# Two-block transformer layer in split float32: interleaving the halves of the held activations, and a different column order, slot shift or weight spread in each column group of the feed-forward

## What is computed

```python
def second_block(x, mem, ...):
    h = rms_norm(x, norm_mix_g);  x = x + hybrid_mixer(h, ...)
    h = rms_norm(x, norm_x_g);    x = x + cross_attention(h, mem_n, w_xq, w_xkv, w_xo)
    h = rms_norm(x, norm_ffn_g)
    x = x + jnp.square(jax.nn.relu(h @ w_ff1)) @ w_ff2     # w_ff1 2048 x 8192, w_ff2 8192 x 2048
    return rms_norm(x, norm_final_g)
```

## Time and profile before

| | us |
|---|---|
| two timed runs | 2842.70, 2843.13 (median 2842.91) |
| the profiled execution, as timed | 2842.74 |
| its span, first to last instruction | 2841.0 |
| around the span | 1.7 |
| TensorE matmul busy | 2822.8 (99%) |
| TensorE weight load busy | 2443.4 (86%) |
| VectorE busy | 1931.6 (68%) |
| ScalarE busy | 1352.2 (48%) |

### The profile page before, as it was taken

One profiled execution on the slowest core, in us unless ns is written; L12 is line 12 of the kernel. 1 busy time (PEld: TensorE's weight loads), 2 busy tenths in 40 slices (PEclk: granted clock), 3 DMA queues, 4 the chain that ended last, 5 costly groups with the idle time before them and its releaser, 6 DMA issues.

```text
span 2841.0 us, 38749 instructions
## 1 busy us (share of the span) xinstructions
PE 2822.8 (99%) x15872; PEld 2443.4 (86%) x15872; DVE 1931.6 (68%) x2513; ACT 1352.2 (48%) x1726; POOL 59.2 (2%) x102
## 2 busy tenths in 40 slices
PE   9999999999999999999999999999999999999998
PEld 8899888888888888888888888888888888888887
DVE  7645557678766668888988875466666555656556
ACT  5433654347344436555555543444345443444434
POOL 0000210000000000000000000000000000000000
PEclk9999999999999999999999999999999999999999
DMA  7454344565555544444343445554455445554443
GB/s 279 181 191 155 142 178 178 185 241 180 196 185 200 185 167 163 148 149 143 140 149 136 159 168 204 178 193 149 148 200 191 187 179 205 190 197 181 192 190 148
DMA packets 72849, 506.66 MB, mean 178 GB/s; under 512 B 8384, under 2 KB 8512, under 8 KB 12896
## 3 DMA queue, kind: packets, MB, share of 16 engines
q1 hardware_dynamic: 71136, 497.83, 47.4%
q0 software_dynamic: 1104, 5.90, 0.6%
q10 hardware_dynamic: 432, 0.45, 0.0%
HBM read 499.95 MB, written 2.10 MB: 177 GB/s over the span
## 4 chain that ended last, share of the span: by engine, by line
PE 92%; DVE 5%; ACT 1%; issue 1%; DMA 1%; SPq 0%; POOL 0%; DVEq 0%; ACTq 0%
PE double L1376 85%; PE bank L1376 6%; DVE wlo L2076 1%; DVE cacc L2082 1%; PE bank L1379 1%; DVE cst L2099 0%; ACT whi L1734 0%; DVE AA L2082 0%; DVE cst L2076 0%; DVE cacc L2079 0%; DMA vec<-in_vec 0%; DVE Cm L2076 0%; DMA raw<-in_wall 0%; DVE Tn L2590 0%; DVE acc L2076 0%
## 5 line engine op out<-in xcount | busy, mean ns | idle before, releaser
L1376 PE MATMUL double<-AA,whi 128*128 128x512 f32 (+1 forms) x5008 | 1641.8, 380 | 3.3 <-DVE wlo L2076 3.2
L1734 ACT ACTIVATE whi<-raw 128x1024 fp32r<-128x1024 f32 x926 | 925.7, 1049 | 833.1 <-PE double L1376 794.9
L1376 PE MATMUL double<-AA,wlo 128*128 128x256 f32 (+1 forms) x4624 | 1299.1, 281 | 0.0
L2076 DVE TENSOR_TENSOR wlo<-raw,whi 128x1024 fp32r<-128x1024 f32 (+1 forms) x934 | 1101.1, 1214 | 200.6 <-ACT whi L1734 198.3
L1376 PEld LDWEIGHTS double<-AA,whi 128*128 128x128 f32 x5008 | 915.4, 188 | 180.1 <-DVE wlo L2076 5.0
L1376 PEld LDWEIGHTS double<-AA,wlo 128*128 128x128 f32 x4624 | 875.4, 189 | 1.4
L1376 PE MATMUL double<-whi,AA 128*128 128x512 f32 x1536 | 488.0, 393 | 0.5 <-DVE wlo L2076 0.5
L1376 PEld LDWEIGHTS double<-whi,AA 128*128 128x128 f32 x1536 | 288.6, 188 | 60.3 <-DVE wlo L2076 0.9
L1376 PE MATMUL double<-whi,BB 128*128 128x512 f32 x1024 | 317.0, 390 | 0.0
L1376 PE MATMUL double<-wlo,AA 128*128 128x512 f32 x768 | 299.4, 390 | 0.0
L1376 PEld LDWEIGHTS double<-whi,BB 128*128 128x128 f32 x1024 | 192.3, 188 | 40.0
(11 more groups left out here) (338 smaller groups left out, 1720.4 us busy)
## 6 DMA issues: line engine op xcount, KB each, us to landing
raw<-in_wall SPq DMA_DIRECT2D x462, 1024.0 KB, 4.8
raw<-in_wall SPq DMA_DIRECT2D x9, 256.0 KB, 6.6
X<-in_xT SPq DMA_DIRECT2D x1, 2048.0 KB, 11.3
Mm<-in_memT POOLq DMA_DIRECT2D x1, 2048.0 KB, 15.6
tmp<-rqk POOLq DMA_DIRECT2D x16, 128.0 KB, 2.2
mblk<-in_memT SPq DMA_DIRECT2D x8, 256.0 KB, 3.4
dec<-in_dec POOLq DMA_DIRECT2D x1, 1536.0 KB, 8.8
hs<-in_hsT SPq DMA_DIRECT2D x4, 272.0 KB, 5.5
```

The costliest lines, as they stand in the source:

```text
L1376: return q.matmul(out, lhsT, rhs, start=start, stop=stop, skip_group_check=True)
L1734: q.activation(hi_of(j)[:, c], raw[j % RAW][:, c], ACT.Copy).then_inc(S("w_hi"), 1)
L2076: return q.tensor_tensor(out, a, b, o)
```

## The change

Nothing is added to or taken from the list of steps. Instruction counts, shapes, waits and transfers are the same. Four things are different:

1. **Layout of the held activations.** `AA` and `BB` are of the same size, but the lo half of a k-tile now lies directly behind its hi half (1,024 bytes further, 1,088 for the 272 tokens of the first block). `AL` is the view with 272 tokens, `AT` the view with 256. The splits on ScalarE and VectorE write into these views; a copy that wrote 512 columns in one run writes two runs of 256.
2. **Slots.** A `whi` slot is 32 elements longer than a unit, a `wlo` slot 48 elements (before: 0 and 64). So the slots' starts move against each other and against `AA`.
3. **f1 groups.** `FEATURE_WAYS` gives each (b, j) but (0, 0) an order of the moving columns of the 512-column matmul, one of the 256-column matmul, a spread of the held weights (`rows`) and the two shifts of the weights in their slots. Order (s, r) walks a row of columns as `(b s r) -> s b r`: runs of r neighbouring columns, one of every s such runs in turn. Moving operand and PSUM output are walked alike, so that each sum is the same. With `rows` 2 or 8 the weights of a tile lie 2 or 8 elements apart, and the array `wall` in DRAM is laid out for that.
4. **f2 groups.** `TOKEN_WAYS` gives each (b, j) an order of the moving weight columns (all but five have one, 27 of 32) and two shifts.

```diff
+NONE = (None, (0, 0))
+PLAIN = (None, None, None, (0, 16))
+FEATURE_WAYS = {
+    (0, 1): (None, (4, 8), None, (0, 16)), (0, 2): ((4, 8), None, None, (0, 16)), (0, 3): ((4, 8), (4, 8), None, (0, 16)),
+    (1, 0): ((4, 8), (4, 16), None, (0, 16)), (1, 1): ((4, 8), (2, 8), None, (0, 16)), (1, 2): ((4, 8), (8, 8), None, (0, 16)), (1, 3): ((4, 8), (4, 4), None, (0, 16)),
+    (2, 0): ((4, 8), (8, 4), None, (0, 16)), (2, 1): ((4, 8), (16, 8), None, (0, 16)), (2, 2): (None, (4, 16), None, (0, 16)), (2, 3): (None, (2, 8), None, (0, 16)),
+    (3, 0): (None, (8, 8), None, (0, 16)), (3, 1): ((16, 8), None, None, (0, 16)), (3, 2): ((2, 8), (4, 8), None, (0, 16)), (3, 3): ((4, 4), (4, 8), None, (0, 16)),
+    (4, 0): ((8, 4), (4, 8), None, (0, 16)), (4, 1): ((16, 4), (4, 8), None, (0, 16)), (4, 2): ((32, 4), (4, 8), None, (0, 16)), (4, 3): ((32, 8), (4, 8), None, (0, 16)),
+    (5, 0): ((4, 8), (4, 8), None, (0, 0)), (5, 1): ((4, 8), (4, 8), None, (0, 32)), (5, 2): ((4, 8), (4, 8), None, (0, 48)), (5, 3): ((4, 8), (4, 8), None, (16, 16)),
+    (6, 0): ((4, 8), (4, 8), None, (32, 32)), (6, 1): ((4, 8), (4, 8), None, (8, 8)), (6, 2): (None, None, None, (8, 24)), (6, 3): ((4, 8), (4, 16), None, (32, 48)),
+    (7, 0): (None, None, 2, (0, 16)), (7, 1): ((4, 8), (4, 8), 2, (0, 16)), (7, 2): ((4, 8), (4, 8), 8, (0, 16)), (7, 3): (None, None, 8, (0, 16)),
+}
+TOKEN_WAYS = {}
+for n, way in enumerate(((None, (0, 0)), ((4, 8), (0, 0)), ((4, 8), (16, 0)), ((4, 8), (32, 0)), ((4, 8), (24, 0)), ((4, 8), (0, 16)), ((4, 8), (0, 32)),
+                         ((4, 8), (0, 48)), ((4, 8), (16, 16)), ((4, 8), (32, 32)), ((4, 8), (24, 24)), ((4, 8), (8, 8)), ((4, 8), (8, 24)), ((4, 8), (4, 4)),
+                         (None, (16, 16)), (None, (32, 32)), (None, (0, 32)), (None, (8, 8)), ((4, 4), (0, 0)), ((8, 4), (0, 0)), ((16, 4), (0, 0)),
+                         ((32, 4), (0, 0)), ((64, 4), (0, 0)), ((32, 8), (0, 0)), ((2, 2), (0, 0)), ((16, 8), (16, 16)), ((2, 8), (16, 16)), ((8, 8), (16, 16)),
+                         ((4, 16), (16, 16)), ((2, 16), (8, 8)), ((4, 8), (2, 2)), ((4, 8), (0, 0)))):
+    TOKEN_WAYS[divmod(n, 4)] = way
...
-    whi = [ar.get([P_, UNIT + 0], F32R, f"whi{i}") for i in range(SPL)]
-    wlo = [ar.get([P_, UNIT + 64], F32R, f"wlo{i}") for i in range(SPL)]
+    whi = [ar.get([P_, UNIT + 32], F32R, f"whi{i}") for i in range(SPL)]
+    wlo = [ar.get([P_, UNIT + 48], F32R, f"wlo{i}") for i in range(SPL)]
...
-    AA = ar.get([P_, 2, NT * L], F32R, "AA")
-    Ahi, Alo = AA[:, 0, :], AA[:, 1, :]
+    AA = ar.get([P_, 2 * NT * L], F32R, "AA")
+    AL = AA[:, :].rearrange("p (k s n) -> p k s n", s=2, n=L)
+    AT = AA[:, 0:2 * NT * T].rearrange("p (k s n) -> p k s n", s=2, n=T)
...
-    BB = ar.get([P_, 2, 8 * T], F32R, "BB")
+    BB = ar.get([P_, 8, 2, T], F32R, "BB")
...
     def set_off(j):
         pr = P.pairs[units[j][0]]
+        if pr["tag"] == "f2":
+            return TOKEN_WAYS.get(pr["idx"], NONE)[1]
+        if pr["tag"] == "f1":
+            return FEATURE_WAYS.get(pr["idx"], PLAIN)[3]
         return (0, 16 if pr["kind"] == "T" else 0)
...
+        def walk(way, x):
+            return x if way is None else x.rearrange("p (b s r) -> p s b r", s=way[0], r=way[1])
...
                     elif kind == "N":
-                        o = out[:, m * 512:(m + 1) * 512]
-                        mm_group(o, hh[:, cs], wh[:, i, :], start=first, stop=False)
-                        mm_group(o, hh[:, cs], wl[:, i, :], start=False, stop=False)
-                        ins = mm_group(o, hl[:, cs], wh[:, i, :], start=False, stop=last)
+                        way = TOKEN_WAYS.get(pr["idx"], NONE)[0] if pr["tag"] == "f2" else None
+                        o, h_, l_ = walk(way, out[:, m * 512:(m + 1) * 512]), walk(way, wh[:, i, :]), walk(way, wl[:, i, :])
+                        mm_group(o, hh[:, cs], h_, start=first, stop=False)
+                        mm_group(o, hh[:, cs], l_, start=False, stop=False)
+                        ins = mm_group(o, hl[:, cs], h_, start=False, stop=last)
+                    elif pr["tag"] == "f1":
+                        long, short, rows, _ = FEATURE_WAYS.get(pr["idx"], PLAIN)
+                        o, s_ = out[:, m * 512:(m + 1) * 512], out[:, m * 512:m * 512 + T]
+                        wh_, wl_ = wh[:, i, cs], wl[:, i, cs]
+                        if rows == 2:
+                            wh_, wl_ = (x[:, i, :].rearrange("p (c m) -> p m c", m=2)[:, m, :] for x in (wh, wl))
+                        if rows == 8:
+                            wh_, wl_ = (x.rearrange("p (a c n) -> p a n c", a=2, n=8)[:, half, 2 * (i % 4) + m, :] for x in (hi_of(j), lo_of(j)))
+                        mm_group(walk(long, o), wh_, walk(long, flat(both)), start=first, stop=False)
+                        ins = mm_group(walk(short, s_), wl_, walk(short, hh), start=False, stop=last)
```

More of the change, by code:

```diff
@@ L1331, in A2 @@
     def A2(t, j):
-        return t[:, 2 * j * T:2 * (j + 1) * T]
+        return AT[:, 2 * j:2 * j + 2, t, :]
     def XT2(j, m):
@@ L1383, in operand @@
             if pr["ready"][0] == "b_lo":
-                return BB[:, :, a * T:(a + 1) * T]
+                return BB[:, a, :, :]
             if pr["kind"] == "W":
[L1386 to L1391, removed]
+                return AL[:, a, :, :]
+            if pr["tag"] in ("gp", "q", "mp", "ga", "ma"):
+                return AL[:, a, :, META:L]
+            return AT[:, a, :, :]
+        def walk(way, x):
+            return x if way is None else x.rearrange("p (b s r) -> p s b r", s=way[0], r=way[1])
         def mm(key):
@@ L1758, in s_a1 @@
                 q.wait_ge(S(f"hs{HS[k]}"), 16)
-            q.activation(Ahi[:, k * L:(k + 1) * L], hs[:, k, :], ACT.Copy, scale=V("norm_gain", k)).then_inc(S("a_hi"), 1)
+            q.activation(AL[:, k, 0, :], hs[:, k, :], ACT.Copy, scale=V("norm_gain", k)).then_inc(S("a_hi"), 1)
         def s_sq0(j, r):
@@ L1782, in b_hi @@
         def b_hi(i, r):
-            q.activation(flat(Bhi[:, 2 * i:2 * i + 2, :]), tmps[r["t"]][:, :], ACT.Copy).then_inc(S("b_hi"), 1)
+            q.activation(BB[:, 2 * i:2 * i + 2, 0, :], two(tmps[r["t"]][:, :]), ACT.Copy).then_inc(S("b_hi"), 1)
         def s_mix(g, r):
@@ L1824, in s_a2 @@
             q.wait_ge(S("merged"), at["au", k]["m"])
-            q.activation(A2(Ahi, k), flat(Macc[:, 2 * k:2 * k + 2, :]), ACT.Copy).then_inc(S("a_hi"), 1)
+            q.activation(A2(0, k), Macc[:, 2 * k:2 * k + 2, :], ACT.Copy).then_inc(S("a_hi"), 1)
         def s_nrm(key, r):
@@ L1874, in f @@
                 q.wait_ge(S("ev"), at["res", (r["res"], k // 2)]["ev"])
-                q.activation(Ahi[:, k * T:(k + 1) * T], X[:, k, :], ACT.Copy, scale=scale(k)).then_inc(S("a_hi"), 1)
+                q.activation(AT[:, k, 0, :], X[:, k, :], ACT.Copy, scale=scale(k)).then_inc(S("a_hi"), 1)
             return f
@@ L1977, in s_memn @@
             q.wait_ge(S("w_used"), r["used"])
-            q.activation(Ahi[:, k * T:(k + 1) * T], mblk[k // 2][:, k % 2 * T:(k % 2 + 1) * T], ACT.Copy,
+            q.activation(AT[:, k, 0, :], mblk[k // 2][:, k % 2 * T:(k % 2 + 1) * T], ACT.Copy,
                          scale=V("norm_mem_g_2", k)).then_inc(S("a_hi"), 1)
@@ L1995, in s_a4 @@
             q.wait_ge(S("w_used"), r["used"])
-            q.activation(A2(Ahi, j), flat(Macc2[:, 2 * j:2 * j + 2, :]), ACT.Copy).then_inc(S("a_hi"), 1)
+            q.activation(A2(0, j), Macc2[:, 2 * j:2 * j + 2, :], ACT.Copy).then_inc(S("a_hi"), 1)
         def s_x_s(h, r):
@@ L2008, in s_a6 @@
             q.wait_ge(S("xat_vec"), at["x_o", (j // 2, j % 2)]["o"])
-            q.activation(A2(Ahi, j), flat(Mx[:, 2 * j:2 * j + 2, :]), ACT.Copy).then_inc(S("a_hi"), 1)
+            q.activation(A2(0, j), Mx[:, 2 * j:2 * j + 2, :], ACT.Copy).then_inc(S("a_hi"), 1)
         def s_f1(i, r):
@@ L2115, in s_a1 @@
             q.wait_ge(S("a_hi"), r["hi"])
-            c = slice(k * L, (k + 1) * L)
-            stt(Alo[:, c], hs[:, k, :], V("norm_gain", k), Ahi[:, c].bitcast(F32), ALU.mult, ALU.subtract).then_inc(S("a_lo"), 1)
+            stt(AL[:, k, 1, :], hs[:, k, :], V("norm_gain", k), AL[:, k, 0, :].bitcast(F32), ALU.mult, ALU.subtract).then_inc(S("a_lo"), 1)
         def s_sq0(j, r):
@@ L2180, in b_lo @@
             q.wait_ge(S("b_hi"), r["hi"])
-            hi = flat(Bhi[:, 2 * i:2 * i + 2, :]).bitcast(F32)
-            tt(flat(Blo[:, 2 * i:2 * i + 2, :]), tmps[r["t"]][:, :], hi, ALU.subtract).then_inc(S("b_lo"), 1)
+            hi = BB[:, 2 * i:2 * i + 2, 0, :].bitcast(F32)
+            tt(BB[:, 2 * i:2 * i + 2, 1, :], two(tmps[r["t"]][:, :]), hi, ALU.subtract).then_inc(S("b_lo"), 1)
         def s_mix(g, r):
@@ L2275, in f @@
                 q.wait_ge(S("a_hi"), r["hi"])
-                tt(A2(Alo, j), src(j), A2(Ahi, j).bitcast(F32), ALU.subtract).then_inc(S("a_lo"), 1)
+                tt(A2(1, j), src(j), A2(0, j).bitcast(F32), ALU.subtract).then_inc(S("a_lo"), 1)
             return f
@@ L2281, in f @@
```

(18 more changed lines are left out.)

2 lines of the change are left out of this document (removed).

## The result

The changed kernel takes 2900.0 us (2898.36 and 2901.64) against 2842.91: 1.020 times as long, with a 95% interval of 1.0183 to 1.0217. I had forecast 2855. The time lies inside the range I gave, but the loss is 57 us where I expected 12. That the change costs time is clear of the noise; whether it costs more than 2% is not. The profiled execution has a span of 2896.6 us, 55.6 more than before.

The account below looks back on a forecast made before the run. TensorE was taken as the bound from end to end, so only matmul pace could matter. 2842.7 + 5.8 (slots) + 3.1 (f1's sweep) + 3.5 (spread weights) = 2855 us, other terms 0; range 2818 to 2935.

Parts of the forecast that it names:

- The bound: Whole kernel: TensorE bounds it end to end, PE busy 99%, so only the time of one matmul can matter.
- What would show it: Profile after: feed-forward blocks 86 to 91 us, f1 groups under 12 except weights 8 apart, walked matmuls within 10 ns.
- Term 1: Hi and lo halves side by side in AA and BB: 0 us, bound -13 us.
- Term 2: New slot lengths, matmuls outside the feed-forward: +5.8 us from moved T pairs at +3.4 ns, N matmuls 0.
- f1's sweep of places: Shifts and steps in f1 average like gp: +3.4 ns on 900 pairs, +3.1 us.
- Term 3: Walked columns in f1 and f2: run boundaries taken as 0; f1's sweep +3.1 us, f2 0.
- Term 4: Spread held weights in f1 (7, 0) to (7, 3): 256 matmuls wait for slower loads, +3.5 us, from 0 to +14.
- Rival A: Walked feed-forward matmuls: each run boundary costs one column time, 0.417 ns, +77.5 us in all, 2932; chance 0.21.
- Rival B: Feed-forward walks keep moving columns and weight loads apart, half the surplus goes, -24 us, 2828; chance 0.19.

Follow-up runs that it names:

- the layout alone: Changed kernel with halves side by side but old slots and no walks, shifts or spreads: 2844.01 us, ratio 1.0003 to the kernel before.
- the first probe: Changed kernel with old slots, each feed-forward group given one case: walks on moving side, PSUM side or both, or cut held tiles; run once, 2909.85 us.
- the walked kernels: Changed kernel with old slots, no spreads: one-run T groups walked, 2808.79 us; N matmuls walked too, 2803.31; nine N groups plain again, 2795.71.

## Why the prediction was right and wrong

- **The bound** was right: PE is at 99% in both kernels, no other engine is over 1 us busier, and all of the 55.6 us is pace of matmuls.
- **What would show it** said no: the feed-forward blocks 4 to 7 took 93.0, 94.5, 100.8 and 105.0 us and not 86 to 91, f1 (4, 1) and (4, 2) took over 12 us with plain held weights, and walked matmuls differed by far over 10 ns from unwalked ones.
- **Term 1, halves side by side, 0**: right, shown by the layout alone (44.37 us for the wo groups, as before).
- **Term 2, slots, +5.8**: right for the T pairs (5.2 measured outside the feed-forward) and in its pattern, since slot 2 stayed at 346.7 ns and the other two rose. The closeness of the number is partly luck: a moved pair of wo costs 4.8 or 4.3 ns and not 3.4, and groups among small products lose less. The term was mis-sized for N. I put N at 0 because no row shows another place; it was 5.1 us outside and 4.0 inside. With f1's 2.8 (I had 3.1 for f1's sweep of places), the slots came to 16.4 us against 9. The rule behind it, the place modulo 256 bytes, is not enough: f1 (5, 0) of the first probe, in plain order, has its weights at the same places modulo 256 as slot 0 here (hi 0, lo 192) and runs at 346.6 ns, slot 0 at 351.5. What it is about the place stays open.
- **Term 3, walked columns, 0**: this is the step that failed. I held that a run boundary costs nothing, and counted boundaries, where lines count. For most groups 0 was nearly right: (4, 4) on old slots is 226.5 ns, (4, 8) 230.6. But runs of 2 cost 11.0 us, the shift by half a line 6.2 (both by lines, as the probe shows), and the ten groups with longer steps 11.8, which touch no line more and whose cause is open: 29 us in twelve groups. A sweep is not its mean: a few bad cases outweigh all the others, since a good case can win at most the 13 ns above the columns and a bad one can lose 230.
- **Term 4, spread weights, +3.5**: mis-sized, 9.0. I let the 512 matmul cover its load. The pace is that of the loads: the timeline of f1 (7, 3) of the changed kernel shows loads of 0.33 us, one right behind the other,

```profile
2822.54 0.33 PEld L1400 LDWEIGHTS double<-AA,whi 128*128 128x128 f32 x1
2822.76 0.34 PEld L1400 LDWEIGHTS double<-AA,wlo 128*128 128x128 f32 x1
2823.02 0.33 PEld L1400 LDWEIGHTS double<-AA,whi 128*128 128x128 f32 x1
```

  two of them every 0.48 us (0.347 for a pair before). Half of the 487.6 ns of a pair is 244 ns a load, 30 above the 213 of 128 lines. My price was one wait of 110 ns a pair, 7 us, of which I took half; it left out that a load of 244 ns is longer than the 512 matmul too (230). That makes 127 ns of wait for one matmul and 14 for the other, 141 in all, as measured. By the starts of the matmuls, 129 ns of it stand between the 512 matmul and the 256 one behind it and 12 behind that. The Trainium skill's rule for lines ("SBUF — State Buffer", section "Door 1: The DMA port swizzle") picked the right groups here: 2 apart, with two hits in a line, cost 0.2 us a group, 8 apart 4.5.
- **Rival A, 2932**: wrong in its mechanism though its side (slower) was right. The price of 0.417 ns a boundary is refuted by (4, 4), 127 boundaries and not one ns. The block that it named as the longest, block 5, took 94.5 us, less than blocks 6 and 7 (100.8 and 105.0). The sentence of the Trainium skill that backed it ("SBUF — State Buffer", section "Door 1: The DMA port swizzle"), that any non-contiguous PSUM pattern significantly slows matmuls, does not hold here for float32 runs of 2 and more: 10.88 us a group against 10.89.
- **The two hits per line** that the Trainium skill asks for (same section), taken alone, would make runs of 2 free on the read side. Here they double the time, 453 to 461 ns against 227, since both visits of a line are paid, and the measurement decides.
- **Rival B** failed for the changed kernel as a whole, but half of the surplus can go, as the walked kernels show. Its reason, and mine for the surplus, that moving columns and weight loads collide, is not supported in f2, where the surplus stays with a quarter of the load, and open in the T pairs, whose pace depends on the slot of the held weights.

## What to carry to other kernels

Count the lines of 16 bytes that a matmul's moving and held operands touch, each visit for itself, before counting anything else: on the moving side a line is worth four columns of 2.4 GHz (1.7 to 1.8 ns measured), and a run of 2, or an 8-byte offset together with runs of 8 or 16, shows up in full. An 8-byte offset without a walk adds one line and costs little (234 ns against 227). The PSUM side could be walked in every order tried, in runs of 2, 4 and 8, at no cost. Where TensorE is the bound, orders and shifts that keep the lines were worth 1.2 to 1.7% here, and other slot lengths cost 0.6%, but they must be measured in the place where they will stand, behind the neighbours that they will have; a table with one case per group ranks them only roughly.

## What was not expected of the hardware

- The same T pairs at the same addresses run in one of two repeating patterns, 333.5 or 341.6 ns, for tens of microseconds, and the group just before them decides which. (xo holds a third pace, 335.6, in all three kernels.)
- An f2 matmul's surplus above its columns does not shrink with the weight load: 13.5 ns with 128 held columns, 18.6 with 32.
- 64 and 128 bytes in the lengths of the weight slots, with no instruction changed, cost 16.4 us, and the pace of each unit follows its slot.
- For runs of 4 the step between runs matters up to 50 ns a matmul, worst at 256 bytes; its cause is open, as is that of the remaining surplus.
